# Gates by scatter instead of one-hot products, and the U products' two activation halves as one 512-column operand

## What is computed

```python
q = (hf @ w_q).reshape(t, 8, 2, 128)
s1 = jnp.einsum('thd,nd->thn', q[:, :, 0], sk[0])
s2 = jnp.einsum('thd,nd->thn', q[:, :, 1], sk[1])
v1, i1 = lax.top_k(s1, 16)
v2, i2 = lax.top_k(s2, 16)
cand = (v1[..., :, None] + v2[..., None, :]).reshape(t, 8, 256)
cs, ci = lax.top_k(cand, 16)
row = jnp.take_along_axis(i1, ci // 16, axis=-1)
col = jnp.take_along_axis(i2, ci % 16, axis=-1)
experts, gates = row * 128 + col, jax.nn.softmax(cs, axis=-1)
a = jax.nn.gelu(jnp.einsum('chkd,cd->chk', expert_u[experts], hf))
out = jnp.einsum('chk,chkd->cd', gates * a, expert_v[experts])
```

## Time and profile before

| what | value |
|---|---|
| time, median of 3 | 3389.89 us (3389.41 to 3393.11) |
| the profiled execution's own time | 3403.4 us |
| its span | 3401.7 us |
| mean granted TensorE clock | 0.969 |
| TensorE busy | 3173.4 us (93%) |
| VectorE busy | 1994.0 us (59%) |
| ScalarE busy | 1479.0 us (43%) |
| GpSimd busy | 60.5 us (2%) |
| DMA | 591.70 MB, mean 174 GB/s |

### The profile page before, as it was taken

One profiled execution on the slowest core, in us unless ns is written; L12 is line 12 of the kernel. 1 busy time (PEld: TensorE's weight loads), 2 busy tenths in 40 slices (PEclk: granted clock), 3 DMA queues, 4 the chain that ended last, 5 costly groups with the idle time before them and its releaser, 6 DMA issues.

```text
span 3401.7 us, 49402 instructions
## 1 busy us (share of the span) xinstructions
PE 3173.4 (93%) x17240; PEld 2684.7 (79%) x17240; DVE 1994.0 (59%) x3112; ACT 1479.0 (43%) x1862; POOL 60.5 (2%) x109
## 2 busy tenths in 40 slices
PE   7999989889999999999639999999979999989998
PEld 5877767667999999999628888888858877767776
DVE  4466665554679666665474454554555665457754
ACT  3334443343444566665214444444443334345543
POOL 0000000000000000000000000000000000000000
PEclk9999998999999999999869999999989999989999
DMA  6554442454455555555555555555545545543344
GB/s 210 190 190 162 140 145 99 167 193 167 149 183 183 180 199 195 200 197 194 196 182 186 187 189 186 188 187 186 202 162 191 180 157 184 178 140 123 109 136 167
DMA packets 160302, 591.70 MB, mean 174 GB/s; under 512 B 18080, under 2 KB 18128, under 8 KB 158144
## 3 DMA queue, kind: packets, MB, share of 16 engines
q1 hardware_dynamic: 147600, 535.89, 46.8%
q0 software_dynamic: 12592, 54.31, 4.3%
HBM read 569.15 MB, written 20.97 MB: 173 GB/s over the span
## 4 chain that ended last, share of the span: by engine, by line
PE 77%; DVE 6%; ACT 2%; DMA 2%; issue 1%; DVEq 0%; POOL 0%; ACTq 0%; SPq 0%
PE bank L511 10%; PE bank L513 9%; PE bank L512 9%; PE bank L671 7%; PE bank L672 7%; PE bank L673 7%; PE bank L725 7%; PE bank L726 7%; PE bank L727 7%; PE bank L687 2%; PE bank L546 1%; PE bank L480 1%; DMA xt_hi<-gates_scratch 1%; DVE lo L1141 1%; DVE hall L1574 1%; DVE xt_lo L1186 1%
## 5 line engine op out<-in xcount | busy, mean ns | idle before, releaser
L1141 DVE TENSOR_TENSOR lo<-raw,hi 128x1024 fp32r<-128x1024 f32 (+1 forms) x1025 | 1252.4, 1222 | 1258.6 <-ACT hi L854 1243.6
L854 ACT ACTIVATE hi<-raw 128x1024 fp32r<-128x1024 f32 (+1 forms) x1025 | 1083.7, 1057 | 1601.4 <-PE bank L513 884.3
L511 PE MATMUL bank<-hi,xt_hi 128*128 128x512 f32 (+1 forms) x2052 | 825.5, 402 | 25.8 <-DVE xt_lo L1186 13.1
L513 PE MATMUL bank<-hi,xt_lo 128*128 128x512 f32 (+1 forms) x2052 | 804.6, 392 | 0.0
L512 PE MATMUL bank<-lo,xt_hi 128*128 128x512 f32 (+1 forms) x2052 | 803.3, 391 | 0.0
L671 PE MATMUL bank<-xt_hi,hi 128*128 128x256 f32 x2048 | 589.9, 288 | 2.1 <-DVE gate_t L1547 1.4
L672 PE MATMUL bank<-xt_lo,hi 128*128 128x256 f32 x2048 | 579.0, 283 | 0.0
L673 PE MATMUL bank<-xt_hi,lo 128*128 128x256 f32 x2048 | 578.9, 283 | 0.0
L511 PEld LDWEIGHTS bank<-hi,xt_hi 128*128 128x128 f32 x2052 | 388.6, 189 | 156.5 <-DVE lo L1141 41.8
L725 PE MATMUL bank<-hi,w_hi 128*128 128x512 f32 x1024 | 406.5, 397 | 87.9 <-DVE w_lo L1586 83.9
L513 PEld LDWEIGHTS bank<-hi,xt_lo 128*128 128x128 f32 x2052 | 388.4, 189 | 85.3
(11 more groups left out here) (191 smaller groups left out, 1816.7 us busy)
## 6 DMA issues: line engine op xcount, KB each, us to landing
raw<-in_w_u SPq DMA_DIRECT2D x256, 512.0 KB, 3.5
raw<-in_w_v SPq DMA_DIRECT2D x256, 512.0 KB, 3.5
raw<-in_w_ein SPq DMA_DIRECT2D x128, 512.0 KB, 3.5
raw<-in_w_oin SPq DMA_DIRECT2D x72, 512.0 KB, 3.4
raw<-in_w_att SPq DMA_DIRECT2D x64, 512.0 KB, 3.5
raw<-in_w_gate SPq DMA_DIRECT2D x64, 512.0 KB, 3.5
raw<-in_w_out SPq DMA_DIRECT2D x32, 512.0 KB, 3.5
raw<-in_w_qp SPq DMA_DIRECT2D x32, 512.0 KB, 3.5
```

The costliest lines, as they stand in the source:

```text
L511: pe.matmul(acc, xh, h_[:, s], start=first, stop=False)
L513: mm = pe.matmul(acc, xl, h_[:, s], start=False, stop=last)
L854: act.activation(hi[d][:, 0:width], raw[s][:, 0:width], ACT.Copy).then_inc(hi_ready, 1)
L1141: dve.tensor_tensor(lo[d][:, 0:width], raw[s][:, 0:width], hi[d][:, 0:width].bitcast(F32), ALU.subtract)\
```

## The change

It has three parts.

*Gates.* GpSimd zeroes the DRAM scratch at the start, in four stores of 4 MB. `routing()` works head by head, 17 steps a head over 68 tiles; at each head's end it has the cell number (`place`) and the gate (`picked`) of every token and choice, and GpSimd adds the gates into the scratch by 32 indirect DMAs of 128 single words per head, waiting for the head before to have landed. There are no one-hots, gate products, staging or turned lists. The scratch is laid out by tile, and GpSimd loads it in 32 groups of four tiles (512 KB): group 0 to its own buffer once all additions have landed, the others into eight slots in the room of the activations, from the end of U on, as slots come free. VectorE multiplies tile j into GALL one by one (`gate(j)`), in the V stage two tiles ahead.

*U products.* The activations' halves lie side by side (`xt`, k, half, token), and a weight piece's high half is multiplied with both in one product of 512 columns; the low half follows with one of 256. VectorE adds the two halves of the bank into GALL (`add_u`), and gelu is taken there in place. U uses banks 6 and 7; `added` frees them, and the last quarter of V's first tile waits for it.

*Turns.* Nine GEMMs wait, block by block, for the pair of activation pieces that the block needs (`turn0`) instead of for the last pair.

```diff
-ROUTE_TILES, GATE_TILES = 48, 64
+ROUTE_TILES, ROUTE_STEPS, ROUTE_ASK = 68, 17, 10
+GATE_GROUP, GATE_SLOTS = 4, 8
...
+        xt_t = sb("xt", 32 * T, F32R)
+        xt = xt_t[:, :].rearrange("p (k w t) -> p k w t", k=16, w=2)
+        xt_hi, xt_lo = xt[:, :, 0], xt[:, :, 1]
...
+            gp.memset(zero[:, :], 0.0).then_inc(zero_ready, 1)
+            gp.wait_ge(zero_ready, 1)
+            for c in range(4):
+                gp.dma_start(gates_dram[16 * c:16 * c + 16].rearrange("a p c -> p a c"),
+                             zero[:, :].unsqueeze(1).to_broadcast([P, 16, 512])).then_inc(gates_zeroed, 16)
...
+            gp.wait_ge(gates_zeroed, 4 * 16)
+            cells = gates_dram.rearrange("a p (c one) -> (a p c) one", one=1)
+            for h in range(H):
+                if h:
+                    gp.wait_ge(scattered, 16 * 2 * TOPK * h)
+                gp.wait_ge(routed, h + 1)
+                for t in range(2):
+                    for k in range(TOPK):
+                        c = t * P + h * TOPK + k
+                        gp.indirect_dma_start(cells, bass.IndirectOffsetOnAxis(ap=place[:, c:c + 1], axis=0),
+                                              picked[:, c:c + 1], None, compute_op=ALU.add).then_inc(scattered, 16)
+            gp.wait_ge(scattered, 16 * 2 * TOPK * H)
+
+            tiles = gates_dram.rearrange("a p c -> (a p c)").rearrange("(j p t) -> p j t", j=N_EXPERT_TILES, p=P)
+            for n in range(N_EXPERT_TILES // GATE_GROUP):
+                if n == 1:
+                    gp.wait_ge(block_used, FIRST["w_v"])
+                if n > GATE_SLOTS:
+                    gp.wait_ge(gated, GATE_GROUP * (n - GATE_SLOTS + 1))
+                gp.dma_start(GATE_IN[gate_slot(n)], tiles[:, GATE_GROUP * n:GATE_GROUP * n + GATE_GROUP])\
+                  .then_inc(gates_in[gate_slot(n)], 16)
...
+                    if turn0 is not None:
+                        pe.wait_ge(turn_out, min(turn0 + q + 1, turns.n))
...
-                        acc = bank[2 * (g % 2)][:, 0:T]
-                        pe.matmul(acc, h_[:, s], xt_hi[:, k], start=k == 0, stop=False)
-                        pe.matmul(acc, h_[:, s], xt_lo[:, k], start=False, stop=False)
-                        mm = pe.matmul(acc, l_[:, s], xt_hi[:, k], start=False, stop=k == 15)
-                        if gates is not None and kk == 3:
-                            gates(2 * (j % 2) + q, i)
+                        acc = bank[6 + g % 2]
+                        pe.matmul(acc[:, :], h_[:, s], xt[:, k].rearrange("p w t -> p (w t)"), start=k == 0, stop=False)
+                        mm = pe.matmul(acc[:, 0:T], l_[:, s], xt_hi[:, k], start=False, stop=k == 15)
...
+                        if first and q == 1 and t == 1:
+                            pe.wait_ge(added, N_EXPERT_TILES)
...
+                g = GALL[:, j] if i is None else GALL[:, bass.ds(i * 2 + j, 1)].rearrange("p a t -> p (a t)")
+                act.wait_ge(added, j + 1 if i is None else i * 2 + (j + 1))
+                act.activation(g, g, ACT.Gelu_apprx_tanh).then_inc(chunk_out, 1)
+
+            def beside_route(slot):
+
+                h, part = divmod(slot, ROUTE_STEPS)
+                if part == ROUTE_ASK + 2 and h < H:
+                    e = EXPG.rearrange("p (t h) k -> p t h k", t=2)[:, :, h]
+                    act.wait_ge(act_in, gives.next())
+                    act.activation(e, e, ACT.Exp).then_inc(act_out, 1)
...
+            def gate(j):
+                n, g = divmod(j, GATE_GROUP)
+                if g == 0:
+                    dve.wait_ge(gates_in[gate_slot(n)], 16 * gate_round(n))
+                dve.wait_ge(chunk_out, FIRST_CHUNK["w_u"] + j + 1)
+                dve.tensor_tensor(GALL[:, j], GALL[:, j], GATE_IN[gate_slot(n)][:, g], ALU.mult).then_inc(gated, 1)
...
+            def add_u(j, i=None):
+
+                acc = bank[6 + (FIRST_CHUNK["w_u"] + j) % 2]
+                dst = GALL[:, j] if i is None else GALL[:, bass.ds(i * 2 + j, 1)].rearrange("p a t -> p (a t)")
+                b = FIRST["w_u"] + 2 * j + 2
+                dve.wait_ge(block_used, b if i is None else i * 4 + b)
+                dve.tensor_reduce(dst, acc[:, :].rearrange("p (w t) -> p t w", w=2), AX.X, ALU.add).then_inc(added, 1)
...
             for b in range(2 * ROUTE_TILES):
                 split(FIRST["w_u"] + 1 + b)
+                if b and b % 2 == 0:
+                    add_u(b // 2 - 1)
                 next(route, None)
...
+            for j in range(N_EXPERT_TILES):
                 b = FIRST["w_v"] + 2 * j + 1
+                split(b)
+                if j + 1 < N_EXPERT_TILES:
+                    low_weights(j + 1, None)
+                if j + 2 < N_EXPERT_TILES:
+                    gate(j + 2)
+                split(b + 1)
```

More of the change, by code:

```diff
@@ L516, in gemm_chunk, with gemm @@
                         beside(slot + q)
-            def gemm(name, k0=0, head=0, tail=0, beside=None):
+            def gemm(name, k0=0, head=0, tail=0, beside=None, turn0=None):
                 n, nb = GEMMS[name]
@@ L523, in gemm @@
                 for c in range(head):
-                    gemm_chunk(name, c, None, 0, k0)
+                    gemm_chunk(name, c, None, 0, k0, turn0=turn0 if c == 0 else None)
                 if loops:
@@ L530, in gemm @@
                     slot = (c - (n - tail)) * nb
-                    gemm_chunk(name, c, None, 0, k0, W, beside if slot >= 0 else None, slot)
+                    gemm_chunk(name, c, None, 0, k0, W, beside if slot >= 0 else None, slot,
+                               turn0 if c == 0 else None)
             def attention_steps(k):
@@ L657, in _, with expert_u @@
             pe.wait_ge(score_out, 8)
-            def expert_u(j, i, gates=None):
+            def expert_u(j, i):
                 g = FIRST_CHUNK["w_u"] + j
-                pe.wait_ge(chunk_out, g - 1 if i is None else i * 2 + (g - 1))
+                if i is None and j < 2:
+                    pe.wait_ge(chunk_out, FIRST_CHUNK["w_u"])
+                else:
+                    pe.wait_ge(added, j - 1 if i is None else i * 2 + (j - 1))
                 for q in range(2):
@@ L778, in beside_ein @@
                     turn_pair(pairs("conv_g")[slot - 70])
-            gemm("w_ein", tail=10, beside=beside_ein)
+            gemm("w_ein", head=2, tail=10, beside=beside_ein, turn0=first_h3)
             pe.wait_ge(tm_ready, ready.next())
@@ L1460, in _, with top16 @@
             dve.wait_ge(score_out, 8)
-            def top16(n, v, v2, val, idx, size):
-                for first in range(0, n, 2 * size):
-                    for k in range(first, first + 2 * size):
-                        ins = dve.max(val[:, k, 0:8], v[:, k])
+            def top16(lists, v, v2, val, idx):
+                for n, k in lists:
+                    ins = dve.max(val[:, k, 0:8], v[:, n])
+                done(ins)
+                yield
+                half = len(lists) // 2
+                for part in (lists[:half], lists[half:]):
+                    for n, k in part:
+                        dve.max_index(idx[:, k, 0:8].bitcast(U32), val[:, k, 0:8], v[:, n])
+                        ins = dve.match_replace(v2[:, n], val[:, k, 0:8], v[:, n], NEG)
@@ new lines, in top16 @@
+                for n, k in lists:
+                    ins = dve.max(val[:, k, 8:16], v2[:, n])
+                done(ins)
+                yield
+                for n, k in lists:
+                    ins = dve.max_index(idx[:, k, 8:16].bitcast(U32), val[:, k, 8:16], v2[:, n])
+                done(ins)
+                yield
+            of_head = lambda v, h: v.rearrange("p (t h) k -> p t h k", t=2)[:, :, h]
+            of_half = lambda v, h, half: v.rearrange("p (t h x) k -> p t h x k", t=2, x=2)[:, :, h, half]
@@ new lines, in routing @@
+            def routing():
+                done(dve.tensor_tensor(PICK_P, ident[:, :], iota[:, :], ALU.mult))
+                done(dve.tensor_reduce(token[:, 0:1], PICK_P, AX.X, ALU.add))
+                done(dve.tensor_scalar(token[:, 1:2], token[:, 0:1], float(P), None, ALU.add))
+                for h in range(H):
+                    n = 0
+                    for _ in route_head(h):
+                        n += 1
+                        yield
+                    while n < ROUTE_STEPS:
+                        n += 1
+                        yield
@@ L1579, in low_weights @@
+            gate(0)
+            gate(1)
             def low_weights(j, i):
```

330 lines of the change are left out of this document (119 added, 211 removed).

## The result

The changed kernel takes 3237.4 us (median of 4 runs, 3230.3 to 3242.9); the kernel before, run beside it, 3391.5 (3389.4 to 3398.7). The ratio is 0.9541, 95% interval 0.9517 to 0.9565: 154 us faster. The forecast was 3226 within 3200 to 3270. The profiled execution after took 3237.1 us with a span of 3235.3. Its page and rows follow, beside those of before.

A forecast was written before the change was run, and what follows sets the result against it. TensorE, busy 93% of the span, was taken to bound the kernel. Savings of 188.6 us less 25 added gave 164 net; 3403.4 - 164 - 13.5 (profiled execution above median) = 3226 us, range 3200 to 3270.

The forecast's parts named there:

- the wide product: U: three products of 256 columns per k become one of 512 and one of 256, 2.773 us a block; 27.3 us less.
- Gates out of U and the hand-over: U: gate products removed from 128 blocks, 56.3 us less; the wait after routing for softmax and lists removed, 6.4 us less.
- the hole: Between U and V: TensorE's idle time of 83.9 us goes; 1 us added for V's start.
- V at the full clock: V's start: about eight products no longer run at half speed, 0.2 us each; 1.6 us less.
- V's pitch: U: the 512-column product costs 0.233 us as in V, not the GEMM's 0.227; saving 13.7 us less, time 3240.
- VectorE: U while routing: blocks with both a sum and a heavy routing part run late; 7 us added.
- ScalarE: U while routing: eight exponentials' table loads delay copies, losing 0.85 or 1.25 us, four of each; 8 us added.
- `turn0`: Nine GEMM starts: TensorE waits for each turn instead of the last, saving 1.45 us each; 13.1 us less.
- The clear: Kernel start: GpSimd's clearing of 16.8 MB delays weight loads; 5 us added, bounds 0 and 30.
- The gate reads beside V: V's start: eight groups of gates read at once, 4.2 MB; 4 us added, bounds 0 and 11.
- The additions: U: 256 indirect additions on GpSimd at 1.2 us each, bounds 0.54 and 3.9, hidden with 300 us to spare.
- The threshold of c = 2.5: Slow-scatter rival, chance 0.08: gates complete 82 + 256 c after U starts; from c = 2.5 us per issue V waits.

The follow-up runs named there:

- experiment 8: Changed kernel with the last 103 indirect additions each waiting for a VectorE subtraction's end, in two tries (second three blocks later): 3234.2 and 3229.1 us, one execution each.
- experiment 2: Changed kernel with U's products again three of 256 columns per k and without VectorE's sum per tile: 3261.0 us, ratio 0.9601 to the kernel before.
- experiment 4: Changed kernel with the exponential in routing's eight softmaxes replaced by the already loaded gelu, so the output differs: 3231.1 us, ratio 0.9521 to the kernel before.
- experiment 1: Changed kernel with each GEMM again waiting at its first product for the last of its four turns: 3258.2 us, ratio 0.9603 to the kernel before.
- experiment 9: Changed kernel with GpSimd's seven loads at V's end spread over tiles 98 to 124, at most 1 MB at a time: 3234.9 us, ratio 0.952.
- experiment 7: Changed kernel with GpSimd waiting after each of the 256 indirect additions until it has landed: 3560.9 us, one execution.
- experiment 5: Changed kernel with each U block's eight wide products first, then its eight narrow ones: 3235.2 us, one execution.
- experiments 1 to 4: Changed kernel with, in turn: turn waits undone, three products in U, clear spread in 32 stores, routing without table loads: 3258.2, 3261.0, 3231.0, 3231.1 us.
- experiments 5 to 11: Later edits of the changed kernel: product order, halves apart, additions singly, additions delayed, loads spread, 18 blocks per head, four edits together; 3216.4 (last) to 3560.9 us.

## Why the prediction came out as it did

The forecast was 11 us low: the medians differ by 154 us, and the sum's net was 164. With each term at what the runs show (the parts below), the net is 153 to 156. The term that missed is the wide product, 13.7 us too high; the errors of the others nearly cancel. That the profiled executions agree with the sum (3403.4 - 164 = 3239, measured 3237) is luck: 8 us of their 166 are the clock in attention's stretch, which before's execution had lost and after's had not. The 13.5 us lead from before's profiled execution to its median, where the sum had to end; no trace of another execution tells how much of them that clock makes. By parts:

- **Gates out of U and the hand-over** (56.3 + 6.4) and **the hole** (83.9 less 1). From U's first product to its last before took 796.7 us, 59.5 more than 256 blocks of 2.88, so the first two are 59.5, not 62.7. From U's last product to V's first it was 84.2 us and is 1.1: 83.1. With 13.6 for the wide product, less 10.9 of stalls, that is the 145.3 of the table; the prediction's terms make 157.9 of it.
- **V at the full clock** (1.6): right in kind, and nearer 3. V's first fourteen products took up to 0.2 us more each before, of which one of 0.1 is left.
- **The wide product** (27.3) was mis-sized. Its sign of being right, U blocks at 2.77 us outside routing, failed: they took 2.827. It gives 13.6 at this pace, and 27.3 would be right at the other (experiment 8). The prediction named V's pitch with 13.7 as the alternative, and the GEMM's was the wrong choice for most of U. That it pays at all experiment 2 shows: U's products are 12 us longer without it, and the additions' pace adds 11.
- **VectorE** (7) and **ScalarE** (8). Stalls take 10.9 us of U, not 15. 5 are the table loads (experiment 4), which leaves 6 for VectorE. The sum costs 0.68 us as taken. Where the exponential follows the second split the loads cost 1.2 to 1.5 us, as the 1.25 of the prediction had it; where it follows the first they cost nothing, and not 0.85.
- **`turn0`** (13.1): nine gaps, 16 us by the rows, 13 by the stages (experiment 1).
- **The clear** (5): 8.6. Its bound of 30 was worked out from the 13.4 us of the earlier trace rows as if TensorE had stood still for them (it stood still for some 4, experiment 9), and so was too high. The Trainium skill's rule (DMA: Bandwidth & Descriptors, Queues, rings and completion order), which I took to mean a cost near 30, is not borne out in size: with DMA at 0.93 of its time from 35 to 100 us, ScalarE waited 14.5 us for weights.
- **The gate reads beside V** (4): nothing. V is 660 of 660 us busy, at 204 GB/s where it had 187.
- **The additions**: 2.07 us each, not 1.2, and 36 to 40 us to spare, not 300. The conclusion (hidden) held; the margin did not. The threshold of c = 2.5 was the right quantity: the additions started 2.50 us apart on the mean. By the formula the gates are then complete 722 us after U's start; they were at 690 (1555.6, when GpSimd goes on to the first load of gates), since the formula charges the landings twice, and V starts at 736. Nothing in the trace of before showed what the issue shares with VectorE.

## What to carry to other kernels

A hidden stage needs its margin stated in the terms that set it: here most of GpSimd's issues behind routing fall into step with VectorE's subtractions, one per weight block, and what is taken from the rest of U comes off their margin. Read what a late transfer costs from the gaps of the engine that needs it, never from the length of a DMA row in the chain. Check a sum of changes term by term, and not by its total: here two profiled executions agreed with it within 3 us although one term was 14 off, because a clock that dips in some executions lay between them.

## What the runs showed of the hardware

- An indirect addition of 128 words takes GpSimd 1.54 us alone (84 of 84 in experiment 7). Begun 0.1 to 1.1 us behind the start of a subtraction of VectorE with two operands in SBUF it ends 1.42 us behind the subtraction's end, which makes up to 2.5 us; begun ahead of it, or behind its end (experiment 8), it takes 1.54, and the subtraction takes 1.22 to 1.25 all the same.
- The same pair of products (512 and 256 columns) ran at 0.3467 or 0.3533 us, in stretches of up to 340 us of one execution (experiment 8 against the changed kernel). What sets it at a hiccup stays open.
- Alternating, a product of 512 and one of 256 columns cost 0.353 us in most blocks; eight wide and then eight narrow cost 0.349 per pair (experiment 5); three of 256 cost 0.360 (experiment 2).
- The granted clock in attention's stretch (560 to 580 us) was 0.57, 1.00, 0.69, 0.66, 0.63 and 1.00 in the executions of before, after and experiments 1 to 4, worth up to 9 us. The edits of 2 and 4 lie behind that stretch and have 0.66 and 1.00, so the edit isn't what decides; no run tells what does. On the chip of experiments 5 to 11 all eight had 1.00, and no edit was profiled on both chips.
